# Moving a two-layer decoder step's small elementwise products from GpSimd to VectorE

## What is computed

```python
proj = rmsnorm(x) @ w_in                      # z (2048), x/B/C (3072), dt (32 heads)
xBC = silu(causal_dwconv(xBC, conv_buf, conv_w) + conv_b)     # 4 taps
# prompt rows, in chunks of 128 (ssd_chunked):
chunk_states = einsum("bcsgn,bcsge,bcsgep->bcgepn", Bc, decay_to_end, xd)
h = h_prev * chunk_decay + chunk_states       # over 4 chunks
y = (C B^T * decay) @ xd + C @ h_prev * exp(a_cum)
# sample rows, one token each, the same recurrence:
h = exp(dt * A) * h + dt * x * B ;  y = h @ C
y = (y + D * xs) * silu(z)
y = y * rsqrt(mean(y * y, per group of 512 channels) + eps) * norm_w
out = y @ w_out
```

## Time and profile before

| | |
|---|---|
| three runs | 1032.13, 1032.26, 1034.06 us |
| median | 1032.26 us |
| span of the profiled execution, first to last instruction | 1030.7 us |
| busy in the span: TensorE / VectorE / ScalarE / GpSimd | 913.2 / 658.9 / 482.2 / 480.9 us |
| mean granted TensorE clock | 0.946 of full speed |

### The profile page before, as it was taken

The page is one execution under the profiler, slowest core; times in us unless marked ns, Lnnn a source line. Parts: engine busy times, 40 slices in busy tenths (PEclk is TensorE's granted clock), DMA queues, the critical chain, the costliest instruction groups (busy, mean ns, idle before and its releaser), DMA issues.

```text
span 1030.7 us, 20709 instructions
## 1 busy us (share of the span) xinstructions
PE 913.2 (89%) x7371; PEld 891.6 (86%) x7371; DVE 658.9 (64%) x908; ACT 482.2 (47%) x897; POOL 480.9 (47%) x233
## 2 busy tenths in 40 slices
PE   5869796967797879659999999999999999989996
PEld 5669696967787878559999999999999999989996
DVE  5668997998799889987654643333334433354653
ACT  5456645763576366673344432333232332333344
POOL 6324674467347745745341644344434343333420
PEclk8889898989898989779999999999999999989999
DMA  7125442644354453413231432322333333322212
GB/s 190 45 82 176 138 128 82 189 128 127 91 159 129 129 167 109 141 42 103 89 94 42 123 102 81 102 81 84 99 94 89 90 93 87 96 81 75 90 60 83
DMA packets 158834, 108.01 MB, mean 105 GB/s; under 512 B 5024, under 2 KB 146876, under 8 KB 158204
## 3 DMA queue, kind: packets, MB, share of 16 engines
q1 hardware_dynamic: 119780, 76.15, 25.1%
q10 hardware_dynamic: 38592, 30.54, 9.9%
q0 software_dynamic: 400, 0.55, 0.3%
HBM read 95.35 MB, written 12.14 MB: 104 GB/s over the span
## 4 chain that ended last, share of the span: by engine, by line
PE 55%; DVE 27%; issue 7%; ACT 3%; DVEq 2%; POOL 1%; ACTq 0%; POOLq 0%
PE bank L1250 37%; PE bank L1409 18%; DVE acc L915 9%; DVE st L979 3%; DVE ybuf L956 2%; DVE yr L983 2%; DVE zh L990 2%; DVE hs L946 1%; DVE dtx L973 1%; DVE ybuf L997 1%; DVE xd L929 1%; DVE xs L924 1%; ACT thx L576 1%; DVE yob L963 1%; ACT acc L570 1%
## 5 line engine op out<-in xcount | busy, mean ns | idle before, releaser
L352 POOL TENSOR_TENSOR wlo<-raw,whi 128x1024 fp32r<-128x1024 f32 x136 | 338.0, 2485 | 419.0 <-ACT whi L489 410.2
L1250 PE MATMUL bank<-hhi,whi 128*128 128x260 f32 x1664 | 343.5, 288 | 14.6 <-ACT ext L566 12.5
L1250 PE MATMUL bank<-hlo,whi 128*128 128x260 f32 x1664 | 338.9, 286 | 0.0
L1250 PE MATMUL bank<-hhi,wlo 128*128 128x260 f32 x1664 | 338.8, 286 | 0.0
L1250 PEld LDWEIGHTS bank<-hhi,whi 128*128 128x128 f32 x1664 | 261.2, 192 | 19.1 <-ACT ext L566 14.8
L489 ACT ACTIVATE whi<-raw 128x1024 fp32r<-128x1024 f32 x136 | 143.7, 1056 | 250.3 <-PE bank L1250 153.5
L1250 PEld LDWEIGHTS bank<-hlo,whi 128*128 128x128 f32 x1664 | 260.7, 192 | 0.0
L1250 PEld LDWEIGHTS bank<-hhi,wlo 128*128 128x128 f32 x1664 | 260.4, 191 | 0.0
L1078 DVE TENSOR_TENSOR hlo<-ybuf,hhi 128x520 fp32r<-128x520 f32 x64 | 85.5, 1369 | 55.1 <-ACT hhi L732 55.0
L915 DVE SCALAR_TENSOR_TENSOR acc<-ext,colA,acc 128x544 f32<-128x544 f32 x72 | 102.7, 1427 | 21.3 <-ACT acc L570 12.3
L1409 PE MATMUL bank<-hhi,whi 128*128 128x260 f32 x512 | 105.3, 288 | 4.7 <-DVE hlo L1078 4.7
(11 more groups left out here) (212 smaller groups left out, 1146.8 us busy)
## 6 DMA issues: line engine op xcount, KB each, us to landing
raw<-in_sc_w_in SPq DMA_DIRECT2D x64, 512.0 KB, 4.0
raw<-in_ssd_w_in SPq DMA_DIRECT2D x40, 512.0 KB, 3.9
abc<-a_rows ACTq DMA_DIRECT2D x16, 512.0 KB, 3.8
st<-in_state_ssm ACTq DMA_DIRECT2D x16, 512.0 KB, 5.3
out_new_ssm_s<-st ACTq DMA_DIRECT2D x16, 512.0 KB, 3.6
raw<-in_ssd_w_out SPq DMA_DIRECT2D x16, 512.0 KB, 3.8
raw<-in_sc_w_out SPq DMA_DIRECT2D x16, 512.0 KB, 3.8
bcbc<-bc_rows ACTq DMA_DIRECT2D x4, 1024.0 KB, 7.2
```

Of the source, the lines that this page charges most:

```text
L352: pool.tensor_tensor(wlo[:, slot, :], raw[:, slot % RAW, :], whi[:, slot, :].bitcast(F32), ALU.subtract).then_inc(lo_done, 1)
L1250: mm = pe.matmul(b[:, 0:TH], w[:, slot, k * P:(k + 1) * P], h[:, k, cols], start=(k == 0 and i == 0), stop=(k == KT - 1 and i == 2))
```

## The change

The GpSimd stream of the loop keeps the ten low parts and nothing else. `weigh`, `inject`, `read_out` and `add_squares`, word for word the same operations on the same buffers, are put into VectorE's stream, each at one place: `weigh` behind `weigh_dt`, `inject` ahead of `sample_add`, `read_out` ahead of `sample_out`, the first two `add_squares` behind `gate(1)` and `gate(2)`, the last two at the end of the group. No data moves otherwise, and ScalarE's, TensorE's and SyncE's streams are the same.

```diff
@@ gpsimd, before the loop over groups @@
             pool.sem_inc(lo_done, SLOT)
-            pool.sem_inc(sqs_done, 1)
...
-            pool.wait_ge(sqs_zero, 1)
             with pool.Fori(0, GROUPS // 2) as G:
                 for gg in range(2):
-                    g = group_half(G, gg)
-
                     def next_low(m):
 
                         i = gg * 10 + m
                         pool.wait_ge(proj_done, G * 20 + (i + 1))
                         low(G * 20 + (i + SLOT), i % SLOT, G * 160 + ((i + SLOT) // RAW + 1) * 16)
 
-                    def weigh(q):
...
-                    next_low(0)
-                    next_low(1)
-                    next_low(2)
-                    weigh(0)
-                    next_low(3)
-                    next_low(4)
-                    weigh(1)
-                    next_low(5)
-                    inject(0)
-                    read_out(0)
-                    weigh(2)
-                    inject(1)
-                    next_low(6)
-                    read_out(1)
-                    next_low(7)
-                    weigh(3)
-                    add_squares(0)
-                    inject(2)
-                    read_out(2)
-                    next_low(8)
-                    inject(3)
-                    add_squares(1)
-                    read_out(3)
-                    next_low(9)
-                    add_squares(2)
-                    add_squares(3)
+                    for m in range(10):
+                        next_low(m)
@@ vector @@
             dve.sem_inc(silu_done, 1)
+            dve.sem_inc(sqs_done, 1)
...
             dve.wait_ge(dt_s, 10)
+            dve.wait_ge(sqs_zero, 1)
...
+                    def weigh(q):
+                        dve.wait_ge(xd_done, g * 4 + (q + 1))
+                        scale = dte[:, :, ds(g * 8 + 2 * q, 2)].unsqueeze(3).broadcast_to([P, NC, 2, HD])
+                        dve.sem_inc(turnstile_p, 1)
+                        dve.tensor_tensor(xdd[:, :, :].rearrange("p c (h d) -> p c h d", h=2),
+                                           xd[:, :, :].rearrange("p c (h d) -> p c h d", h=2), scale, ALU.mult).then_inc(xdd_done, 1)
+
+                    def inject(q):
+                        dve.wait_ge(dtx_done, g * 4 + (q + 1))
+                        dve.wait_ge(yr_done, g * 4 + (q + 1))
+                        if q == 0:
+                            dve.wait_ge(bcbc_in, g * 16 + 16)
+                        dve.tensor_tensor(tdec[:, :, :], bcbc[:, :, 0, :], dtx[:, q % 2, :].unsqueeze(2).broadcast_to([P, NB, NS]),
+                                           ALU.mult).then_inc(t1_done, 1)
+
+                    def read_out(q):
+                        dve.wait_ge(st_new, g * 4 + (q + 1))
+                        dve.tensor_tensor(tdec[:, :, :], st[:, q % 2, :].rearrange("p (b n) -> p b n", n=NS),
+                                           bcbc[:, :, 1, :], ALU.mult).then_inc(t2_done, 1)
+
+                    def add_squares(q):
+                        if q < 3:
+                            dve.wait_ge(sq_done, g * 3 + (q + 1))
+                        else:
+                            dve.wait_ge(gate_done, g * 4 + (q + 3))
+                            dve.wait_ge(sqs_done, g * 4 + (q + 1))
+                            yt = ybuf[:, ds(g * 4 + q, 1), :].squeeze(1)
+                            dve.sem_inc(turnstile_p, 1)
+                            dve.tensor_tensor(sqb[:, :], yt, yt, ALU.mult).then_inc(sqp_done, 1)
+                            dve.wait_ge(sqp_done, g + 1)
+                        if q > 0:
+                            dve.wait_ge(sqs_done, g * 4 + (q + 1))
+                        ss = sqs[:, ds(g, 1), :].squeeze(1)
+                        dve.sem_inc(turnstile_p, 1)
+                        dve.tensor_tensor(ss, ss, sqb[:, :], ALU.add).then_inc(sqs_done, 1)
...
                     weigh_dt(0)
+                    weigh(0)
...
                     weigh_dt(1)
+                    weigh(1)
...
                     skip(1)
+                    inject(0)
                     sample_add(0)
                     weigh_dt(2)
+                    weigh(2)
                     sample_x(1)
                     silu(5, xs[:, 1, :])
                     causal(2)
+                    read_out(0)
                     sample_out(0)
                     add_earlier(1)
+                    inject(1)
                     sample_add(1)
...
                     weigh_dt(3)
+                    weigh(3)
+                    read_out(1)
                     sample_out(1)
                     causal(3)
                     gate(1)
+                    add_squares(0)
                     add_earlier(2)
+                    inject(2)
                     sample_add(2)
                     recur(3)
                     skip(3)
                     sample_x(3)
+                    read_out(2)
                     sample_out(2)
                     silu_z(2)
                     add_earlier(3)
+                    inject(3)
                     sample_add(3)
                     gate(2)
+                    add_squares(1)
                     silu_z(3)
+                    read_out(3)
                     sample_out(3)
                     gate(3)
+                    add_squares(2)
+                    add_squares(3)
```

## The result

The changed kernel takes 1037.9 us at the median of six runs (1035.3 to 1039.1), the kernel before 1032.9 over six (1031.9 to 1034.2). The ratio is 1.0046, with a 95% interval of 1.0033 to 1.0058: 0.5% slower, 4.7 us, between 3.4 and 6.0. The forecast was 1040.9 us, + 8.6 against the span before, with a range of 1026 to 1055. The profiled execution took 1038.3 us with a span of 1036.5, 5.8 us more than the span before.

A forecast was written before the change was run, and what follows sets the result against it. VectorE was taken to bound the four groups. Each group: + 17.6 added, - 13.65 holds returned, - 1.4 low parts, + 2.6 us; with + 0.9 at the end, + 8.6 on the 1030.7 span, 1040.9 us at the median, range 1026 to 1055.

The forecast's parts named there:

- The bound: In the four groups VectorE is busy 349 of 393 us; a microsecond added there is mostly one more in the time.
- The returned holds: VectorE, each group: thirteen delays by GpSimd's work other than low parts go, 13.65 us less.
- the split by kind: Holds on VectorE going per group: 3.9 us with add_squares, 2.1 with weigh, 7.6 with inject and read_out.
- The added steps: VectorE, each group: injects 5.4, read-outs 5.4, weighings 3.3, squares and sums 3.5, together 17.6 us more.
- The low parts' places: z0 to z3 and the next group's first low part hold VectorE 7.4 us for 8.8, 1.4 less a group.
- the first rival: Those five low parts mostly miss VectorE's holdable instructions: about 1014 us with no delay left, 1025 with two; chance 0.13.
- The end of the last group: From last gate to output projection 6.0 us for 5.6, the gate itself 0.5 later: + 0.9 us.
- The sum: + 2.6 us a group, + 7.7 over groups 0 to 2, + 0.9 in the last: + 8.6, 1040.9 us.
- that the whole hold comes back: All GpSimd time removed returns to VectorE, -32 + 17.6 us a group: about 975 us; chance 0.02.
- that all come to stand in full: Five low parts each hold VectorE 2.3 us, plus 1 us of issue: + 7.7 a group, about 1060; chance 0.17.
- that it comes out even: Something else sets a good part of the group, or the ledger is off by 2 us: 1032 us; chance 0.13.

The follow-up runs named there:

- the cut widths: Kernel before with GpSimd's weigh, inject, read_out, squaring and sum of squares cut to 8 or 1 columns: 988.1 us, ratio 0.9564.
- the low parts (53 and 65): Low parts cut to one column in the loop: 985.1 us from the changed kernel, 967.6 us from the kernel before.

## Why the prediction was right

**The bound.** VectorE sets the group. Shown by the cut widths (45 us back), by the low parts (53 and 65) and by the table above. The change brought no new waits, as forecast; ScalarE and TensorE begin to show in the kernels that lose much of the holds (8.5 to 14 us of waits more where 56 to 79 us of holds are gone).

**The returned holds.** Put at 13.65 us a group. In group 2, on which it was counted, the added steps, 17.2, less the 2.0 us by which the group grew (2.5, of which 0.45 are a wait for TensorE that it hadn't before) and less 1.2 that the low parts gave up, leave 14.0. The cut widths freed 56 us of holds in four groups, 14.0 a group, though only 11.3 showed in the time. And the 31 us of holds a group, which the prediction compared with the 76 us of three lines alone, are the 124 us of all lines. The sum for the whole change was sound; the split by kind was not, as the moves of `add_squares` (1.6 us a group for 3.9) and of `inject` and `read_out` (11.9 for at most 9.6) showed.

**The added steps.** 17.6 forecast. The eight large products cost 0.10 us less each than put down, 0.8 us a group, and the weighings 0.08 more each, 0.3 a group, and the squares 0.05: 17.2. A dependent step of 1024 columns takes 1.25 us, where I had carried over the 0.22 us that the taps of 544 columns showed. The increments and register instructions that were put at nothing don't show: an added sum of squares steps in 0.61 us (328.28 to 328.89), as put down.

**The low parts' places.** All five came out within 0.1 us of the list in group 2. What was too large was to take that group for all: behind the branch B's low part held 0.9 us and not 2.3, and x2's, which was to stay as it was, held 1.2 us in group 1 and 1.0 in group 3 (1.9 and 2.2 before). The first is a bit of the first rival (a low part that falls into the idle time at the branch), in one of three group ends.

**The end of the last group.** + 0.9 forecast, of which 0.5 up to the gate and 0.4 behind it. From its silu of C to its gate the last group was 0.8 us shorter and the way from the gate to the projection 1.3 longer: + 0.5. Neither part came out as put down; that their sum did is luck.

**The sum.** + 1.7 a group three times, + 0.5, and 0.4 less ahead of group 0: the projection starts 5.2 us later in the profile (455.71 for 450.53), the runs give 3.4 to 6.0, the forecast was 8.6. It was too high by about 4 us, because over the loop 2.5 us more of holds went than it said (62.7 for four times 13.65 + 1.4) and 1.6 us less was added (68.8, with 2.3 behind the last gate, for 70.4). Of the rivals, the low parts that mostly miss are excluded by the five places, of which only z2's is free; that the whole hold comes back, by the 988 us with that work all but gone; that all come to stand in full, by z2's again; and that it comes out even, by the interval, 3.4 to 6.0 us. The page of the Trainium skill (SBUF — State Buffer, section "SBUF: two separate sides") says that only a VectorE instruction in a two-port mode or with two SBUF inputs is in the contest. The rows agree: recurrence, scaling and reduce (278, 678 and 1220 ns on average in the changed kernel) were never held, taps, adds and the 8-column product were.

## What to carry to other kernels

When an elementwise operation can go on GpSimd or VectorE, don't compare durations: on the full engine's timeline count the time for which GpSimd's instructions held VectorE, and do it for the whole new order at once, since taking work out of GpSimd's stream moves up all that stands behind it (the parts singly gave + 5.8, + 5.6 and 0, the whole + 4.7). Work that must stay on GpSimd is cheap where VectorE reads PSUM, reduces or waits. Semaphore waits that put five low parts of a group there were worth 21 us, over four times what the choice of engine was. And count more than one group: what overlaps what can differ from one to the next.

## What was not expected of the hardware

An add of 128 x 8 elements was held as long as one of 128 x 1024: by 2.2 us, for 0.17 alone (at 349.55 us in the kernel that moves `add_squares`; the large one at 310.86 in the kernel before). And the gap behind an instruction whose result the next one reads isn't a constant: 0.22 us behind the scaling from PSUM, 0.15 behind a tap, but 0.03 behind a 1024-column product (277.13, 355.74 and 303.87 us in the changed kernel).
